# A streamed two-block transformer on one core: low parts of weight chunks in two halves, and one of two convolution groups moved from VectorE to ScalarE and GpSimd

## The reference, cut to what matters

```python
def mixing_layer(h, ...):                      # once for each of the 2 layers
    u = jnp.einsum("bsd,de->bse", h, w_in)     # 1024 -> 2816, that is 22 tiles of 128 columns
    a_b, a_c, a_x, q, k, v, c_in = jnp.split(u, offs, axis=-1)
    y_a = a_b * causal_depthwise_conv(a_c * a_x, short_conv_w)       # 3 taps
    ...                                        # rope on q and k, differential attention of 4 heads
    o = diff_attention(q, k, v, lam)
    o = rmsnorm(o, diff_subln_g) * (1.0 - lam_init)
    c = c_in + glu_b
    c = c[..., :256] * jax.nn.sigmoid(c[..., 256:])
    c = causal_depthwise_conv(c, conf_dw_w) + conf_dw_b              # 31 taps, 256 channels
    y_c = jax.nn.silu(layernorm(c, conf_ln_g, conf_ln_b))
    y = jnp.concatenate([y_a, y_b, y_c], axis=-1)
    return jnp.einsum("bse,ed->bsd", y, w_out)
```

## Time and profile before

| | us |
|---|---|
| median of 3 runs (2060.65 to 2063.24) | 2060.94 |
| the profiled execution | 2065.62 |
| its span, first to last instruction | 2063.5 |

### The profile page before, as it was taken

How to read it: one execution, slowest core, us unless ns; L and a number is a source line. 1 busy time by engine, 2 the same in 40 slices (tenths; PEclk the granted TensorE clock), 3 DMA queues, 4 the chain that set the end, 5 groups by cost and what they waited for, 6 DMA issues and landing times.

```text
span 2063.5 us, 28122 instructions
## 1 busy us (share of the span) xinstructions
PE 1951.3 (95%) x8702; PEld 1530.2 (74%) x8702; DVE 1096.0 (53%) x1399; ACT 692.2 (34%) x1085; POOL 755.2 (37%) x317
## 2 busy tenths in 40 slices
PE   6999999999999999888999999999798999999997
PEld 4776668788888887556778888887565778888885
DVE  5668644478886215886444444123878444444313
ACT  4135553332332222333332323223243333223222
POOL 2321124434444443212334444444221334444443
PEclk9999999999999999999999999999899999999998
DMA  5211112222222332111222222232111122222332
GB/s 207 77 62 40 44 52 97 87 89 94 97 96 94 110 102 72 52 51 51 72 82 93 100 92 101 102 102 84 52 50 52 61 82 95 98 93 100 102 102 81
DMA packets 48654, 173.76 MB, mean 84 GB/s; under 512 B 5456, under 2 KB 6480, under 8 KB 48080
## 3 DMA queue, kind: packets, MB, share of 16 engines
q1 hardware_dynamic: 48592, 172.96, 24.8%
HBM read 169.82 MB, written 2.10 MB: 83 GB/s over the span
## 4 chain that ended last, share of the span: by engine, by line
PE 66%; DVE 6%; DVEq 4%; issue 2%; ACT 1%; ACTq 0%
PE bank L441 21%; PE bank L442 21%; PE bank L461 20%; DVEq L1656 1%; PE bank L452 1%; DVEq L1744 1%; DVE tmp L1745 1%; PE bank L496 1%; PE bank L823 1%; DVE lp L1686 1%; DVEq L1647 1%; DVE small L1677 1%; PE bank L793 1%; DVE conv L1199 1%; DVEq L1609 0%
## 5 line engine op out<-in xcount | busy, mean ns | idle before, releaser
L413 POOL TENSOR_TENSOR wl<-raw,wh x313 | 755.0, 2412 | 1293.9 <-ACT wh L887 1293.9
L441 PE MATMUL bank<-xh,wh 128*128 128x512 f32 x1586 | 643.6, 406 | 28.4 <-ACT wh L887 13.8
L442 PE MATMUL bank<-xl,wh 128*128 128x512 f32 x1586 | 629.9, 397 | 0.0
L887 ACT ACTIVATE wh<-raw 128x1024 fp32r (+1 forms) x313 | 331.9, 1061 | 821.2 <-PE bank L461 785.5
L461 PE MATMUL bank<-xh,wl 128*128 128x512 f32 x1544 | 399.4, 398 | 0.0
L441 PEld LDWEIGHTS bank<-xh,wh 128*128 128x128 f32 x1586 | 305.1, 192 | 104.0 <-DVE sqacc L1214 17.6
L442 PEld LDWEIGHTS bank<-xl,wh 128*128 128x128 f32 x1586 | 305.1, 192 | 67.9 <-issue 5.2
L461 PEld LDWEIGHTS bank<-xh,wl 128*128 128x128 f32 x1544 | 291.7, 191 | 63.1 <-issue 3.5
L1598 DVE TENSOR_TENSOR tmp<-tmp,ybuf 128x512 f32<-128x512 f32 x66 | 180.8, 2739 | 63.8 <-ACT tmp L1086 63.7
L441 PE MATMUL bank<-hh,wh 128*128 128x512 f32 x528 | 208.0, 394 | 0.0
L442 PE MATMUL bank<-hl,wh 128*128 128x512 f32 x528 | 208.0, 394 | 0.0
(11 more groups left out here) (274 smaller groups left out, 1942.1 us busy)
## 6 DMA issues: line engine op xcount, KB each, us to landing
raw<-in_weights SPq DMA_DIRECT2D x313, 512.0 KB, 3.2
xs<-in_x SPq DMA_DIRECT2D x2, 1024.0 KB, 6.1
out_t<-xs SPq DMA_DIRECT2D x8, 256.0 KB, 2.1
w1k<-in_w SPq DMA_DIRECT2D x1, 1024.0 KB, 6.5
w1v<-in_w SPq DMA_DIRECT2D x1, 1024.0 KB, 8.4
shifted<-kvraw SPq DMA_DIRECT2D x8, 124.0 KB, 3.1
posi<-in_positions SPq DMA_DIRECT2D x2, 256.0 KB, 8.6
cst<-in_consts SPq DMA_DIRECT2D x1, 290.0 KB, 8.7
```

The source lines that it names most:

```text
L413: pool.tensor_tensor(wl[:, :, :].rearrange("p s n -> p (s n)")[:, two], raw_slot(t), wh[:, :, :].rearrange("p s n -> p (s n)")[:, two].bit ...
L441: mm(b[:, :], w, kh(k), start=first and k == 0, stop=False)
L442: mm(b[:, :], w, kl(k), start=False, stop=False)
L887: return act.activation(o, i, ACT.Copy, scale=scale)
```

## The change

It has two parts, and the computation stays the same up to the order of the products and sums.

First, `rest` does the low part of a chunk as two GpSimd instructions of 512 columns each; the second raises `lo_ready`. This is for all 313 chunks and the two dummy ones at the end.

Second, in both later layers group 1 of the long convolution leaves VectorE. GpSimd does tap 0 as a multiply with the bias. For k = 1 to 30, ScalarE writes the product (shifted `cpad` times weight) into `tmp[k % 2]` and raises `tap_prod`, and GpSimd adds it to `conv[:, 1]` and raises `tap_added`. GpSimd's loop is written out for the 22 chunks of the stage: from n = 5 on, after the low part of chunk n, two taps. ScalarE does one product at the start of each slot from n = 5 on. A product waits until the add two taps earlier has read its half of `tmp`. TensorE waits for all 30 adds beside `conv_done` in slot s = 26. Group 0 stays on VectorE with the old plan.

```diff
                 v = t.value()
-                two = cols((v % 2) * (CB * P), CB * P)
                 pool.wait_ge(hi_ready, (t + 1).value())
-                pool.tensor_tensor(wl[:, :, :].rearrange("p s n -> p (s n)")[:, two], raw_slot(t),
-                                   wh[:, :, :].rearrange("p s n -> p (s n)")[:, two].bitcast(F32),
-                                   ALU.subtract).then_inc(lo_ready, 1)
-
-            with pool.Fori(0, T_ALL + 2) as t:
+                half = CB * P // 2
+                for h in range(2):
+                    two = cols((v % 2) * (CB * P) + h * half, half)
+                    x_ = pool.tensor_tensor(wl[:, :, :].rearrange("p s n -> p (s n)")[:, two],
+                                            raw[:, cols((v % 4) * (CB * P) + h * half, half)],
+                                            wh[:, :, :].rearrange("p s n -> p (s n)")[:, two].bitcast(F32),
+                                            ALU.subtract)
+                x_.then_inc(lo_ready, 1)
+
+            with pool.Fori(0, T_BLOCK1) as t:
                 rest(Count(0).loop(t, 1))
+
+            with pool.Fori(0, LAYERS) as l:
+                T = Count(T_BLOCK1).loop(l, T_LAYER)
+
+                def tap(k):
+
+                    if k == 0:
+                        pool.tensor_scalar(conv[:, 1, :], cpad[:, 1, 0:S], c2("dw_w", TAPS), c2("dw_b", 1),
+                                           ALU.mult, ALU.add)
+                    else:
+                        pool.drain()
+                        pool.wait_ge(R["tap_prod"], Count(k).loop(l, TAPS - 1).value())
+                        pool.tensor_tensor(conv[:, 1, :], conv[:, 1, :], tmp[:, k % 2, :], ALU.add)\
+                            .then_inc(R["tap_added"], 1)
+
+                for n in range(T_LIN):
+                    if n == 5:
+                        pool.wait_ge(R["glu_out"], Count(1).loop(l, 1).value())
+                    rest(T + n)
+                    if n >= 5:
+                        for k in range(2 * (n - 5), min(2 * (n - 5) + 2, TAPS)):
+                            tap(k)
+                with pool.Fori(T_LIN, T_LAYER) as t:
+                    rest(T.loop(t, 1))
+            for t in range(T_ALL, T_ALL + 2):
+                rest(Count(t))
...
                     if s == 26:
                         pe.wait_ge(R["conv_done"], L1.value())
+                        pe.wait_ge(R["tap_added"], Count(TAPS - 1).loop(l, TAPS - 1).value())
                         ln_stats(U0 + 5, conv)
...
+                def product(k):
+
+                    if k == 1:
+                        act.wait_ge(R["glu_out"], L1.value())
+                    if k > 2:
+                        act.wait_ge(R["tap_added"], Count(k - 2).loop(l, TAPS - 1).value())
+                    copy(tmp[:, k % 2, :], cpad[:, 1, k:k + S], scale=c2("dw_w", TAPS + k)).then_inc(R["tap_prod"], 1)
+
                 for n in range(T_LIN):
-                    for s, steps in layer_slots(n):
+                    for half, (s, steps) in enumerate(layer_slots(n)):
+                        if n >= 5:
+                            k = 2 * (n - 5) + half
+                            if 1 <= k < TAPS:
+                                product(k)
...
-                        for c in range(2):
-                            w = c2("dw_w", c * TAPS + k)
-                            if k == 0:
-                                ts(conv[:, c, :], cpad[:, c, 0:S], w, c2("dw_b", c), ALU.mult, ALU.add)
-                            else:
-                                x_ = fma(conv[:, c, :], cpad[:, c, k:k + S], w, conv[:, c, :])
+                        w = c2("dw_w", k)
+                        if k == 0:
+                            ts(conv[:, 0, :], cpad[:, 0, 0:S], w, c2("dw_b", 0), ALU.mult, ALU.add)
+                        else:
+                            x_ = fma(conv[:, 0, :], cpad[:, 0, k:k + S], w, conv[:, 0, :])
...
+                    if c == 1:
+                        x_.then_inc(R["glu_out"], 1)
```

More of the change, by code:

```diff
@@ L329, in build @@
             "conv_ready", "silu_ready", "prod_ready", "h_hi", "h_lo",
-            "lam_in", "lam_psum", "lam_exp", "lam_ready", "glu_sig", "conv_done",
+            "glu_out", "tap_prod", "tap_added", "lam_in", "lam_psum", "lam_exp", "lam_ready", "glu_sig", "conv_done",
             "qk_ready", "head_normed", "ya_ready", "ln_sub", "ln_sq", "ln_scaled", "yc_ready", "y_hi", "y_lo",
@@ L1668, in glu @@
                     dve.wait_ge(R["glu_sig"], Count(c + 1).loop(l, 2).value())
-                    stt(out=cpad[:, c, TAPS - 1:TAPS - 1 + S], in0=ca[:, c, :], scalar=c2("glu_b", c),
-                        in1=cg[:, c, :], op0=ALU.add, op1=ALU.mult)
+                    x_ = stt(out=cpad[:, c, TAPS - 1:TAPS - 1 + S], in0=ca[:, c, :], scalar=c2("glu_b", c),
+                             in1=cg[:, c, :], op0=ALU.add, op1=ALU.mult)
+                    if c == 1:
+                        x_.then_inc(R["glu_out"], 1)
                 def peak(h, i):
```

## The result

The changed kernel takes 2042.51 us, the median of four runs (2042.14 to 2044.54); the kernel before took 2060.80 beside it (2060.07 to 2063.24). The ratio is 0.9911, with a 95% interval of 0.9894 to 0.9928: 18 us faster, where 43 were forecast. The profiled execution spans 2040.4 us, against 2063.5.

A forecast was written before the change was run, and what follows sets the result against it. VectorE's lateness in some ten places of each projection stage was taken to make TensorE wait and lower its clock. The terms sum to 22.2 us a layer, 44 for two: 2060.9 - 44 = 2017, said as 2018, range 1997 to 2050.

The forecast's parts named there:

- (a): Chunk 4 of the projection stage: take 3.4 us earlier, clock drop behind it gone (3.1), 6.5 us a layer.
- (b): Chunk 6: three pairs of taps become three single ones, 3.5 us of wait and 1.6 of clock, 5.1 a layer.
- (c): The wait of TensorE near 854 us in the projection stage: 1.0 us a layer won.
- (d): Two waits of 2.7 us for later takes: 1.3 each plus one clock drop, 5.7 us a layer; at worst 0.
- (e): The 5.1 us wait for the last head's probability: 3.1 plus 2.4 of clock, 5.5 us a layer; at worst 0.
- a third of 37 us: GpSimd's multiply and 30 adds take 37 us a layer; VectorE was taken to stand still for a third, 12 us.
- the first rival: Contention: adds hold VectorE for half their length, only 7 us a layer is left, 2047 us; chance 0.23.
- The mark that was set in advance: Mean of VectorE's remaining taps: at most 1.1 us for contention as forecast, 1.3 or more for the contention rival.
- (f): Slot 26: a new wait of TensorE for GpSimd's last add, costing 1.6 us a layer.
- The slower rival: Each add holds VectorE for its whole length: 5 to 6 us a layer slower, 2072 us; chance 0.10.
- It doesn't act: TensorE's waits turn to ScalarE's exponentials at the same places: within 4 us of 2061; chance 0.05.
- Everything goes: All takes come in time in the projection stages: 33 us a layer won, 1995 us; chance 0.04.

The follow-up runs named there:

- e1: The kernel before with only the low part cut into two GpSimd instructions, both convolution groups still on VectorE; 2047.91 us.
- e3: The changed kernel with every GpSimd add of a tap cut from 512 columns to 8, so group 1 is not computed; 2010.51 us.
- e2: The changed kernel with the low part in one GpSimd instruction of 1024 columns again, only the new convolution kept; 2059.95 us.
- e7: The changed kernel with both GpSimd's adds and ScalarE's 30 products cut to 8 columns, group 1 not computed; 2010.37 us.
- e12: The changed kernel with each low part in eight pieces of 128 columns and each add of a tap in four; 2004.41 us.
- e10: The kernel before with low parts in eight pieces of 128 columns and VectorE's taps replanned, all taps still on VectorE; 1992.42 us.
- e4: The kernel before with the low part in halves and taps moved from chunks 4 to 6 to 18 and 19, all on VectorE; 2026.88 us.
- e13: The kernel before with low parts in eight pieces of 128 columns and nothing else changed; 2010.14 us.

## Why the prediction was wrong, step by step

**(a) and (b), chunks 4 and 6: right in place and nearly in size.** The wait for chunk 4 fell to 0.3 us, and the stretch behind it is at full clock where it was at 0.66:

```profile
800.00:808.00 8.00, 7.71 (x33) 5.72 (x32) 7.57 (x8) 1.99 (x3) 7.50 (x5) 1.00 0.21 66
```

Forecast 11.6 us a layer; measured 10.7 for the whole change. Of that the split gives 6.9 on top of the halves or 6.4 without them, the halves 3.8.

**(c), (d), (e): the step that failed.** Forecast 12.2 us a layer, measured -0.2 and -0.8. The step that failed is the account of contention on VectorE's path to TensorE's waits: three taps shorter by 2.1, contention longer by only 0.8. The rows that show it are one run of VectorE's work that ends in a take for which TensorE waits. In the kernel before it ran from 873.03 us to 887.82, 14.8 us:

```profile
873.03 0.18 DVE L1219 RECIPROCAL small<-small 128x4 f32<-128x4 f32 x1 [2.34 <-ACT small L904]
...
875.41 2.07 DVE L1745 TENSOR_TENSOR tmp<-ybuf,cos 128x512 f32<-128x512 f32 x1
...
887.14 0.68 DVE L1242 TENSOR_TENSOR ybuf<-bank,rstd 128x512 f32<-128x512 f32 x1
```

The same run in the kernel after, VectorE in order of time:

```profile
855.83 0.18 DVE L1262 RECIPROCAL small<-small 128x4 f32<-128x4 f32 x1 [2.34 <-ACT small L935]
856.10 0.75 DVE L1242 SCALAR_TENSOR_TENSOR conv<-cpad,par,conv 128x512 f32<-128x512 f32 x1
...
857.54 1.70 DVE L1789 TENSOR_TENSOR tmp<-ybuf,cos 128x512 f32<-128x512 f32 x1
...
862.84 1.77 DVE L1691 TENSOR_TENSOR lq<-tmp,tmp 128x512 f32<-128x512 f32 x1
...
864.76 1.22 DVE L1730 TENSOR_SCALAR lp<-lp,small 128x384 f32<-128x384 f32 x1
866.06 1.48 DVE L1242 SCALAR_TENSOR_TENSOR lp<-lp,small 128x384 f32<-128x384 f32 x1
...
870.25 0.68 DVE L1285 TENSOR_TENSOR ybuf<-bank,rstd 128x512 f32<-128x512 f32 x1
```

It takes 15.1 us. The three taps are 2.0 us shorter, nearly as priced. But GpSimd, in the same stretch:

```profile
857.43 1.26 POOL L435 TENSOR_TENSOR conv<-conv,tmp 128x512 f32<-128x512 f32 x1 [2.59 <-ACT tmp L918]
862.79 1.27 POOL L435 TENSOR_TENSOR conv<-conv,tmp 128x512 f32<-128x512 f32 x1 [4.10 <-ACT tmp L918]
864.02 3.10 POOL L415 TENSOR_TENSOR wl<-raw,wh 128x512 fp32r<-128x512 f32 x2
```

The two adds start 0.11 and 0.05 us ahead of a VectorE product and of a sum of two SBUF tiles, and each of these ends 0.55 us after the add: 1.70 in place of 0.69, 1.77 in place of 0.69. Then the two halves hold the two steps of the probabilities, at 1.22 and 1.48 in place of 0.48 and 0.62. The held time of the run is 1.01 + 1.08 + 0.74 + 0.86 = 3.7 us; before it was 1.4. The prediction allowed 0.8 more per wait, and it came to 2.3.

The clock went the same way. Of the three waits before old L793 one was followed by a lower clock (0.60 at 887.96; 1.00 behind the other two). In the changed kernel all three are, 0.77, 0.76 and 0.75 in the 7 to 8 us behind them, 5.1 us in sum against 3.1. The third:

```profile
905.30:912.00 6.70, 6.62 (x22) 4.75 (x23) 6.42 (x6) 2.29 (x5) 5.70 (x4) 0.75 0.00 0
```

(e) failed in its own way. The product that was to be held less (`acp`, 2.76 us before) isn't held at all, but the steps behind it on the way to the last head's probability are: L1799 1.39 in place of 0.49, the two `ya` 3.35 in place of 1.58, L1730 1.25 in place of 0.55, together 3.4 us more. VectorE, then TensorE of the kernel after:

```profile
935.81 0.69 DVE L1797 TENSOR_TENSOR acp<-tmp,tmp 128x512 f32<-128x512 f32 x1
936.58 1.39 DVE L1799 TENSOR_SCALAR ya<-acp,par 128x512 f32<-128x512 f32 x1
938.04 3.35 DVE L1242 SCALAR_TENSOR_TENSOR ya<-acp,par,ya 128x512 f32<-128x512 f32 x2
...
943.67 1.11 PE L846 MATMUL bank<-cst,lp 128*128 128x128 f32 x4 [6.29 <-DVE lp L1242]
```

The wait is 6.3 us where it was 5.1, and the clock behind it is 0.64 from 943.67 to 952 us, where it was 0.73.

Why it is hardly chance: ScalarE's copy of `small` at 855.53 releases VectorE's run at 855.83, and ScalarE's next two instructions, the high part and the product, release the add at 857.43. So the adds come when VectorE has most to do. In the next head the same two adds start 0.11 and 0.04 us ahead of the same two instructions, which again take 1.70 and 1.78. That this order is the cause was not tried by moving the adds. The prediction used it to price the products at nothing, and never asked where it puts the adds.

**Contention: the total near, the place wrong.** From the groups by shape of the stage, less the undisturbed duration of each instruction (0.71 a tap in a pair and 0.75 a tap alone, 0.69 for `cos` and `lq`, 16.0 us for the 32 steps on probabilities), the time that VectorE was held in these four groups, us:

| | taps | `cos` | `lq` | probabilities | sum |
|---|---|---|---|---|---|
| before | 10.9 | 9.0 | 0 | 3.0 | 22.9 |
| e1 | 7.8 | 3.9 | 0 | 6.2 | 17.9 |
| after | 11.9 | 2.1 | 3.5 | 13.3 | 30.8 |
| e3 | 6.8 | 0 | 0.3 | 5.5 | 12.6 |

Rows of the kernel after behind the third line:

```profile
L1242 DVE SCALAR_TENSOR_TENSOR conv<-cpad,par,conv 128x512 f32<-128x512 f32 x30 | 34.4, 1146 | 3.3 <-issue 1.0
L1789 DVE TENSOR_TENSOR tmp<-ybuf,cos 128x512 f32<-128x512 f32 x8 | 7.6, 944 | 0.7
L1691 DVE TENSOR_TENSOR lq<-tmp,tmp 128x512 f32<-128x512 f32 x4 | 6.3, 1585 | 0.4
L1242 DVE SCALAR_TENSOR_TENSOR lp<-lp,small 128x384 f32<-128x384 f32 x4 | 6.0, 1495 | 0.3
```

The prediction took a third of 37 us, 12; the sum rose by 7.9 against before and by 12.9 against e1. The adds alone hold 18.2 (30.8 less 12.6), 46% of their 39.3 us, near the half of the first rival. Four groups that the table leaves out (`yl`, `lk` and the two kinds of `ya` steps) take 3.0 us longer in the changed kernel than in e3, which makes it 54%. The halves had meanwhile lowered what the low part holds. The mark that was set in advance doesn't decide: the taps' mean is 1146 ns, between the 1.1 of the forecast and the 1.3 of the rival. What undid the forecast is the fourth column: 10 us more on the probabilities and 3.5 on `lq`, steps on the way to the waits before L846 and L823. The share from which the third was argued had only the taps and `cos` in it. A tap that is held often costs nothing; a probability that is held costs its whole delay and at times the clock.

**(f), the new wait: right in the first layer, half the cost in the second.** Forecast 1.6 us, measured 1.12 in the first layer, where n = 20 gives back 1.4:

```profile
959.95 1.95 PE L526 MATMUL bank<-cst,conv 128*128 128x1 f32 x16 [1.12 <-POOL conv L435]
```

In the second layer the wait is 1.11 us (at 1586.36), yet chunk 20 gives back 3.0, here and in e2. The clock is lower around it, where the same place of the kernel before has 1.00; after, then before:

```profile
1584.00:1592.00 8.00, 6.88 (x34) 5.72 (x33) 0.82 (x2) 1.77 (x4) 4.26 (x4) 0.79 0.38 131
...
1609.00:1617.00 8.00, 8.00 (x50) 6.91 (x48) 2.29 (x5) 1.77 (x4) 2.35 (x1) 1.00 0.18 66
```

A lower clock behind this wait was priced at nothing.

**Part one: the second mis-sized term.** Forecast 0, from -2 to +2; measured -14.7. The reasoning on turns in the feed-forward was right, and there it is worth nothing. It was the only place at which I looked. In Block 1 and in the projection stages a held product stands close ahead of a matmul that needs it; the halves gained 5.5 us by chunk 39 of Block 1 and 3.8 between n = 4 and n = 7.

**Priced at nothing, and nothing.** The products on ScalarE cost nothing (e7 against e3), and no wait of TensorE for a low part stands among those of after; such waits come only in e12.

**The rivals.** "Contention takes most of it" named 2047 and its mechanism is what e3 showed; without part one, the split gave 2.7 us, less than even this rival's 14. That 2042.5 lies in the range given is luck: the split's 44 us came to 5.4, and the halves' 0 to 14.7. The slower rival needed 57% held; 46 to 54% was measured. "It doesn't act" is refuted by (a). "Everything goes" asks for what only e10 reached.

## What to carry to other kernels

Where GpSimd reads SBUF beside a VectorE that TensorE waits for, look at the length of one GpSimd instruction before its sum: cut it into pieces first, while GpSimd has idle time, and count its queue again at each step (e12). When work is moved to another engine, note which event releases it there; if the same event starts the run of work that is waited for, price the collision at full length on that run, not as a share over the stage. And before moving work at all, try moving it in time: fewer taps ahead of the takes that TensorE waits for (e4) gave more than the move to another engine.

## What was unexpected

- A kernel can gain 52 us while an engine works 522 us more (e13).
- Two colliding VectorE instructions in a row alternate with GpSimd's halves: the first fell from 1740 to 882 ns and the second rose from 680 to 1402, with TensorE's waits for it as before (12.8 and 12.6 us over the execution).
- A step with one SBUF input and a number per partition (L1730, `lp`) is held like the ones with two tiles: 1.22 us in place of 0.48 at 864.76.
- The granted clock of the projection stages hardly rose (0.93 as before in the first, 0.92 to 0.93 in the second): waits of 2.5 to 6.3 us are left, and each that was looked at has a stretch at 0.64 to 0.77 behind it.
